# A two-layer decoder trunk on one core: the raw angle table moves from GpSimd to ScalarE, one projection block changes its PSUM bank, and the order of the recurrent heads is rewritten

## The reference, cut to what matters

```
h = rms_norm(x); proj = h @ w_in            # 1024 -> 512 (u) + 4 x 512 (q, f, i, g)
# mixer A: complex diagonal state space, 32 groups, a = exp(lambda * step)
bu = u @ bbar;  x_t = a * x_{t-1} + bu_t;  y = Re(C x) + d * u;  gelu(y) * sigmoid(gelu(y) @ w_glu)
# mixer B: 4 heads of gated linear recurrence, chunks of 32 tokens
f = lb + (1 - lb) * sigmoid(f);  k = 1 - f;  b = cumsum(log f) in the chunk
scores = (q exp(b - bref)) (k exp(bref - b))^T, causal;  u_chunk = (k exp(blast - b))^T v
state_c = exp(blast) state_{c-1} + u_chunk;  o = scores @ v + (q exp(b)) @ state_{c-1}
x = x + concat(A, rms_norm(o) * silu(g)) @ w_out
```

## Time and profile before

| | us |
|---|---|
| median of three executions | 835.0 (834.51 to 838.63) |
| the profiled execution, its own time | 837.01 |
| its span, first to last instruction | 835.3 |
| PE busy in the span | 773.3 |
| DVE / ACT / POOL busy | 608.6 / 499.8 / 166.1 |
| mean granted TensorE clock | 0.977 of full speed |

### The profile page before, as it was taken

The page is one execution under the profiler, slowest core; times in us unless marked ns, Lnnn a source line. Parts: engine busy times, 40 slices in busy tenths (PEclk is TensorE's granted clock), DMA queues, the critical chain, the costliest instruction groups (busy, mean ns, idle before and its releaser), DMA issues.

```text
span 835.3 us, 11410 instructions
## 1 busy us (share of the span) xinstructions
PE 773.3 (93%) x4356; PEld 579.2 (69%) x4356; DVE 608.6 (73%) x838; ACT 499.8 (60%) x664; POOL 166.1 (20%) x158
## 2 busy tenths in 40 slices
PE   6899999899999899988998999999999899999992
PEld 4587877454688778877876555556579778777771
DVE  5999785887553889887896466667635798787891
ACT  6458422923333488777885118677735488687881
POOL 5320010600001222322211001133101223222121
PEclk9899999999999999999999999999999899999998
DMA  9775554506452599989986300042063599999952
GB/s 368 175 170 128 107 155 85 114 2 252 201 213 116 181 420 362 320 316 327 319 301 217 132 0 1 25 177 101 1 277 151 202 408 352 313 322 329 311 195 39
DMA packets 35403, 170.91 MB, mean 205 GB/s; under 512 B 7841, under 2 KB 10017, under 8 KB 19728
## 3 DMA queue, kind: packets, MB, share of 16 engines
q1 hardware_dynamic: 18432, 130.03, 41.0%
q0 software_dynamic: 15184, 34.56, 17.2%
q10 hardware_dynamic: 1728, 5.52, 1.8%
HBM read 160.18 MB, written 24.12 MB: 221 GB/s over the span
## 4 chain that ended last, share of the span: by engine, by line
PE 42%; DMA 20%; DVE 19%; issue 7%; ACT 7%; POOL 2%; DVEq 1%; ACTq 0%; POOLq 0%
DMA ring<-stream 17%; DVE w_lo L1115 9%; PE PS L2184 8%; PE PS L2433 7%; PE PS L2314 4%; ACT w_hi L760 3%; PE PS L2339 3%; DMA ring_split<-stream 3%; PE PS L2468 2%; PE PS L2131 2%; PE PS L1972 2%; PE PS L1921 2%; DVE arena L1121 2%; PE PS L2214 1%; PE PS L2491 1%
## 5 line engine op out<-in xcount | busy, mean ns | idle before, releaser
L1115 DVE TENSOR_TENSOR w_lo<-ring,w_hi 128x2048 fp32r<-128x2048 f32 x92 | 210.0, 2288 | 41.8 <-ACT w_hi L760 38.0
L760 ACT ACTIVATE w_hi<-ring 128x2048 fp32r<-128x2048 f32 x86 | 164.5, 1916 | 45.1 <-DMA ring<-stream 40.9
L2314 PE MATMUL PS<-w_hi,left_hi 128*128 128x512 f32 x512 | 174.3, 402 | 7.5 <-DVE w_lo L1115 5.3
L2314 PEld LDWEIGHTS PS<-w_hi,left_hi 128*128 128x128 f32 x512 | 96.1, 188 | 30.5 <-DVE w_lo L1115 5.2
L2314 PE MATMUL PS<-w_lo,left_hi 128*128 128x512 f32 x256 | 100.1, 391 | 0.0
L2339 PE MATMUL PS<-w_hi,left_lo 128*128 128x512 f32 x256 | 86.6, 399 | 8.2 <-DVE left_lo L1115 7.0
L2433 PE MATMUL PS<-ring,hT 128*128 128x512 f32 (+1 forms) x192 | 74.7, 534 | 0.0
L608 POOL DMA_INDIRECT arena<-rows x32 | 41.0, 1281 | 125.5 <-PE PS L2291 112.1
L2339 PEld LDWEIGHTS PS<-w_hi,left_lo 128*128 128x128 f32 x256 | 48.8, 190 | 21.3 <-DVE left_lo L1115 9.6
L2433 PEld LDWEIGHTS PS<-ring,hT 128*128 128x128 f32 x192 | 35.2, 193 | 29.3 <-issue 27.6
L2314 PEld LDWEIGHTS PS<-w_lo,left_hi 128*128 128x128 f32 x256 | 48.3, 189 | 8.3
(11 more groups left out here) (301 smaller groups left out, 1479.2 us busy)
## 6 DMA issues: line engine op xcount, KB each, us to landing
ring<-stream SPq DMA_DIRECT2D x110, 1024.0 KB, 16.3
arena<-stream SPq DMA_DIRECT2D x6, 1024.0 KB, 8.2
ring_split<-stream POOLq DMA_DIRECT2D x11, 512.0 KB, 5.6
rows<-arena POOLq DMA_DIRECT2D x8, 512.0 KB, 3.0
x<-stream SPq DMA_DIRECT2D x4, 1024.0 KB, 6.4
x<-x_in SPq DMA_DIRECT2D x4, 512.0 KB, 5.2
ring_split<-stream POOLq DMA_DIRECT2D x2, 1024.0 KB, 8.9
left_lo<-hT_hi POOLq DMA_DIRECT2D x2, 1024.0 KB, 12.1
```

The lines of the kernel that those rows point to most:

```text
L760: act.activation(w_hi[pair], held_slot(layer, m), ACT.Copy).then_inc(w_hi_done, 1)
L1115: return V.tensor_tensor(out, a, b, op)
L2314: ins = mm(PS[:, gate_bank(e), :], a, b, start=k == 0 and t == 0, stop=k == KD - 1 and t == 2)
```

## The change

Four edits, all in layer 0's mixer.

1. The raw angle table is no longer one POOL product but 16 ACT copies of 128x128, each with a column of `turn_hi` as its scale. They stand behind `block_minus(4)` and in front of the evictions of u. DVE waits for `trig_done` instead of `turns_done`.
2. The fourth forget block (`split_proj(3)`) goes to PSUM bank 2 instead of 7 and waits for `u_done` 1 instead of `proj_done` 2. `inputs(0)`, which writes banks 0 to 3, now waits for `proj_done` 4. ACT evicts that block right behind the third, ahead of `block_hi(10)` and of the sine table.
3. PE's order in the second part: `make_taps` and `inputs(1)` one block sooner, `readout(1)` ahead of the last products of value blocks 8 and 9.
4. In the heads, PE runs `head_increments(h+1)` ahead of `head_out(h)`, ACT evicts the keys of head 0 ahead of the exponentials of head 3, and DVE keys head 2 ahead of `states(0)` and head 3 ahead of `states(1)`.

```diff
-            return 3 if i == 2 else 7 if i >= 14 else 6 + i % 2
+            return 5 - i if i in (2, 3) else 7 if i >= 14 else 6 + i % 2
...
-            nc.gpsimd.tensor_tensor(turn_lo, t3, turn_hi, ALU.subtract)
-            pool.drain()
+            nc.gpsimd.tensor_tensor(turn_lo, t3, turn_hi, ALU.subtract).then_inc(turns_done, 1)
             block_lo(1)
-            pool.wait_ge(const_rest, 48)
-            pool.wait_ge(turned_psum, 2 * TT)
...
-            nc.gpsimd.tensor_tensor(cosT.rearrange("p (i c) -> p i c", c=NSTEP), at_step,
-                                    turn_hi.unsqueeze(2).to_broadcast([P, PAIRS, NSTEP]), ALU.mult).then_inc(turns_done, 1)
...
+            act.wait_ge(turns_done, TURN_PARTS)
+            act.wait_ge(const_rest, 48)
+            act.wait_ge(turned_psum, 2 * TT)
+            for pair in range(PAIRS):
+                ins = act.activation(cosT[:, NSTEP * pair:NSTEP * (pair + 1)], con("time")[:, 0:NSTEP], ACT.Copy,
+                                     scale=turn_hi[:, pair:pair + 1])
+            ins.then_inc(trig_done, 1)
...
             projected(2)
+            projected(3)
             block_hi(10)
             block_minus(10)
...
             for h in range(HEADS):
                 exponentials(h)
-            keys_out(0)
+                if h == 2:
+                    keys_out(0)
...
-                if i >= 3:
+                if i >= 4:
                     pe.wait_ge(proj_done, i - 1)
-                if i == 2:
-                    pe.wait_ge(u_done, 2)
+                if i in (2, 3):
+                    pe.wait_ge(u_done, 4 - i)
...
-            pe.wait_ge(proj_done, 3)
+            pe.wait_ge(proj_done, 4)
             pe.wait_ge(bT_done, 2 * STEP)
             inputs(0)
             split_proj(4)
+            make_taps()
             split_proj(5)
-            make_taps()
+            inputs(1)
             split_proj(6)
-            inputs(1)
             split_proj(7)
...
             split_values(9, first)
+            readout(1)
             split_values(8, second)
             split_values(9, second)
-            readout(1)
```

More of the change, by code:

```diff
@@ L333, in trunk @@
                                                                sem("bT_psum"), sem("bT_done"))
-        TURN, RAW = 1, 2
-        TRIG, LB, TABLE = 1, 2, 3
+        TURN, TURN_PARTS = 1, 2
+        TRIG, LB, RAW, TABLE = 1, 2, 3, 4
         BOUNDS, HT_HI, HT_LO, IN_COEF, PHASE, READ_COEF = 1, 2, 3, 5, 6, 7
@@ L555, in _ @@
             pool.drain()
-            nc.gpsimd.tensor_tensor(turn_lo, t3, turn_hi, ALU.subtract)
-            pool.drain()
+            nc.gpsimd.tensor_tensor(turn_lo, t3, turn_hi, ALU.subtract).then_inc(turns_done, 1)
             block_lo(1)
-            pool.wait_ge(const_rest, 48)
-            pool.wait_ge(turned_psum, 2 * TT)
-            at_step = con("time")[:, 0:NSTEP].unsqueeze(1).to_broadcast([P, PAIRS, NSTEP])
-            nc.gpsimd.tensor_tensor(cosT.rearrange("p (i c) -> p i c", c=NSTEP), at_step,
-                                    turn_hi.unsqueeze(2).to_broadcast([P, PAIRS, NSTEP]), ALU.mult).then_inc(turns_done, 1)
             for j in range(2, 12):
@@ L886, in values_hi @@
                 act.activation(v_lo(half), v_hi(half), ACT.Copy, scale=-1.0).then_inc(in_split, 1)
-            for i in range(3, 12):
+            block_hi(11)
+            block_minus(11)
+            for i in range(4, 12):
                 projected(i)
-                if i == 3:
-                    block_hi(11)
-                    block_minus(11)
                 if i in (5, 7):
@@ L1278, in _ @@
             grown(in_b, in_re, in_im, in_tmp, STEP - 1, ALU.subtract, ALU.add).then_inc(coefs_done, 1)
-            dve.wait_ge(turns_done, RAW)
+            dve.wait_ge(trig_done, RAW)
             at_step = con("time")[:, 0:NSTEP].unsqueeze(1).to_broadcast([P, PAIRS, NSTEP])
@@ L1449, in _ @@
             causal(0)
+            keyed(2)
+            decayed(2)
             for h in range(HEADS):
@@ L1453, in _ @@
                     causal(h + 1)
-                if h + 2 < HEADS:
-                    keyed(h + 2)
-                    decayed(h + 2)
+                if h == 0:
+                    keyed(3)
+                    decayed(3)
                 if h:
@@ L2142, in _ @@
             proj(14, low)
+            head_increments(1)
             head_out(0)
-            head_increments(1)
             head_scores(2)
             proj(14, high)
+            head_increments(2)
             head_out(1)
-            head_increments(2)
             head_scores(3)
             proj(15, low)
+            head_increments(3)
             head_out(2)
-            head_increments(3)
             proj(15, high)
```

## The result

The changed kernel takes **826.6 us** (median of four runs, 826.5 to 826.8) against 836.8 us for the kernel before, timed beside it on the same chip (median of four, 834.5 to 838.6): a ratio of 0.988, 95% interval 0.985 to 0.991. The profiled executions say the same: a span of 824.9 us in place of 835.3, an own time of 826.6 in place of 837.0. The forecast was 824.0 with a range of 820 to 830.5.

The account below looks back on a forecast made before the run. PE, busy 93% of the span, was the bound, so gains come from its waits and low clock: 3.3 + 2.9 + 1.2 + 0.95 + 3.0 = 11.4 us off, forecast 824.0 us, range 820 to 830.5.

Parts of the forecast that it names:

- Edit 1: u blocks: without POOL's product `left_lo` comes earlier, 3.3 us, and the clock stays full, 2.9 us; together 6.2 us.
- the point of 33.38 us: u blocks: the moment `left_lo`'s second half arrived in the earlier trace; PE was to pass it at 30.1, 3.3 us sooner.
- Edit 2: Fourth forget block: the 2.04 us wait at `split_proj(3)` goes, `inputs(0)` waits instead; 1.2 us won, bounds nothing and 2.0.
- The late sine table: Ahead of `inputs(1)`: table 4.1 us later, PE still not waiting, by 0.9 us; rival, PE waits, 1 to 3 us, chance 0.06.
- Edit 3: Value blocks 8 and 9: `readout(1)` covers the 1.0 us wait for their low part; 0.95 us won.
- Edit 4: Heads: PE begins `glu` at 198.4 instead of 201.38; 3.0 us won, bounds nothing and 4.5.
- the second way: Heads: waits of 6.7 us become about 5 and 1.7 us of low clock goes; 3.4 us won.
- The clock rivals: u blocks or heads: waits still bring half clock, 827 to 829, chance 0.16; heads staying slow, about 850, chance 0.04.
- All of it reaches the end: Behind the mixer: PE's progress starts the expert weight transfers, so every microsecond won by 218 us reaches the end.
- The sum of 11.4 us: Whole kernel: 3.3 + 2.9 + 1.2 + 0.95 + 3.0 us won, all in layer 0's mixer.
- all 31.9 us of the heads' work at half speed: Heads: the slower case's extreme, clock falling and not rising before `glu`; about 850 us, chance 0.04.
- the good bounds of edits 2 and 4: Fourth forget block and heads: at best 2.0 and 4.5 us won, given as 820.5 us.

Follow-up runs that it names:

- e1_table_only: The kernel before with edit 1 alone (angle table by ACT copies): 830.9 us, ratio 0.991 to 0.997.
- e5_pe_filler: The kernel before plus 22 transposes on PE during its wait for `left_lo`, POOL's table product kept: ratio 0.997 (0.995 to 1.000).
- e12_no_new_order: The changed kernel with edit 3 undone: 824.7 us, ratio 0.982 to 0.993.
- e7: The changed kernel with DVE's old order in the heads: 823.2 us, ratio 0.979 to 0.984.
- e6_pe_heads_old: The changed kernel with PE's old order in the heads (`head_out` ahead of the next increments): 829.0 us, ratio 0.987 to 0.992.
- e9: The kernel before with edit 1 and 16 extra transposes filling PE's wait ahead of `split_proj(3)`: 829.0 us, ratio 0.991 to 0.998.
- e11: The kernel before with edits 1 and 2 only: 829.5 us, ratio 0.988 to 0.995.
- e8: The changed kernel with ACT's old order in the heads (keys of head 0 behind all exponentials): 823.3 us, ratio 0.980 to 0.992.
- e4: The changed kernel with the angle table back on POOL as one product, placed behind `left_lo`: 825.9 us, ratio 0.985 (0.982 to 0.987).
- e10: The changed kernel with DVE's old order in the heads and ACT's gate evictions ahead of head 3's exponentials: 823.8 us, ratio 0.979 to 0.985.
- e3_heads_only: The kernel before with edit 4 alone (order in the heads): 833.6 us, ratio 0.994 to 1.000.

## Why the prediction was right, step by step

**Edit 1: 3.3 us of stall and 2.9 of clock, 6.2; measured 5.6.** Mechanism and place were right: the four products take 0.43 us at 23.92 in place of 3.86, `left_lo` starts at 25.20 (forecast 25.6), and the clock is 1.00 behind the wait. Counted from the first u product, the point of 33.38 us comes 8.10 us behind it in place of 11.01, 2.9 us sooner; and the stage's rest is 2.7 us shorter, the clock. The 0.4 us missing of the stall is a wait of 1.01 us where 0.7 was foreseen: PE began 0.7 us sooner in this execution, DVE only 0.2. The copies took 4.78 us for the 4.8 of the forecast, and PE waited for none of the evictions behind them.

What the prediction did not see is that edit 1 alone can give back 1.6 us at `split_proj(3)`, as it did in the execution of `e1_table_only` (and the filler in `e5_pe_filler`). It took the 1.00 at the 2.0 us wait as a property of that wait. That the sum came out all the same is luck in this point: edit 2 takes the wait away, and with edit 1 alone the same reasoning was wrong by 1.6 us.

**Edit 2: 1.2 us; measured 1.5.** `inputs(0)` waits 0.73 us, the forecast was 0.75. The wait removed was worth 2.29 us from `turn_inputs` to `split_proj(3)` (5.70 to 3.41), not 2.04: PE's start behind a wait costs some tenths too. The late sine table behaved as computed: DVE issued the last of `products_in(1)` by 79.25 + 2.48 = 81.73 us, 15.7 us behind `inputs(0)` (forecast 15.85), and `inputs(1)` came at 83.06, with 1.3 us to spare. That rival did not come about.

**Edit 3: 0.95 us; measured 1.2, and 1.8 by taking it back.** The low part's DMA would have been waited for by 1.6 us in the changed kernel (`e12_no_new_order`), longer than the 1.0 of the earlier trace rows.

**Edit 4: 3.0 us (3.4 by the second way); measured 3.4.** The four waits were foreseen as 0.9, 0.5, 1.75 and 1.6 and are 0.77, 0.62, 1.71 and 1.56. `states(0)` to `states(3)` start 0.5, 1.7, 4.7 and 6.3 us sooner relative to projection 12, for 0.4, 1.3, 4.2 and 5.5. That `states(0)` gains almost nothing was right as well; the prediction stated it as a fact of the change and did not ask what the keying in front costs, and `e7` shows it is 1.5 us.

**The clock rivals.** Neither the 1.0 us wait nor the four of the heads brought the clock down: 1.00 from 150 to 189 us, where the earlier trace rows had 0.59 in one stretch. The Trainium skill, "TensorE: Matmul & The Clock Gate", section "A second HAM failure mode: psum-queue depth-cycling", describes a clock that swings between its two levels when PE is idle for short times between groups of products, often enough; it gives no length for them. In the changed kernel the clock did not swing. In `e6_pe_heads_old`, behind waits of 1.71 us at 157.87 and 1.55 at 163.09, it was 0.83 for 10 us. Waits of the same length stand in the same place in the changed kernel, so the rule does not tell the two apart here.

**All of it reaches the end: not quite.** This is the step that was wrong, by 2.1 us. At the output products PE was 12.5 us ahead, in the end 10.4. The first 1.3 us are lost in the router stage, where PE never waits for long. PE's timeline of the last group of router products and the transposes behind it, before:

```profile
271.70 4.07 PE L2214 MATMUL PS<-param,arena 128*128 128x20 f32 x32
...
278.29 1.29 PE L2247 MATMUL PS<-const 128*128 128x128 f32 x10
```

and in the changed kernel:

```profile
259.17 5.29 PE L2218 MATMUL PS<-param,arena 128*128 128x20 f32 x32
...
267.09 1.58 PE L2251 MATMUL PS<-const 128*128 128x128 f32 x10
```

The work is the same, and the clock was 0.52 for 6 us of it. In the kernel before it was low there too, but less so:

```profile
268.00:276.00 8.00, 8.00 (x68) 7.91 (x67) 6.06 (x12) 4.52 (x7) 1.45 (x3) 0.92 0.60 235
276.00:282.00 6.00, 4.79 (x46) 4.17 (x44) 5.06 (x22) 3.00 (x2) 1.06 (x2) 0.82 0.53 211
```

Length times missing clock gives 1.7 us there and 3.4 in the changed kernel, enough for the 1.3. In the other kernels this stage takes between 68.9 and 70.4 us, and what lies behind it between 543.9 and 549.2 (543.9, 544.0 and 545.5 in `e9`, `e1` and `e11`, 547.0 or more in all others), with no order that the edits explain: `e12`, whose router stage took 69.3 us, and `e8`, 68.9, differ from the changed kernel only in what happens some 60 us earlier and more. I can't say what sets it, and behind the router stage it is not the clock alone: what a low clock costs there, summed over stretches of 10 us, is 8.6 us in the kernel before, 8.5 in the changed one, 8.0 in `e1` (which is 4 to 5 us shorter there) and 6.9 in `e4` (which is as long as the changed one). The spread is as large as an edit of this change, which is the likely reason why the heads' orders and edit 3, which stand clear of each other in their stages, hardly do in the medians.

The sum of 11.4 us was thus met by 11.8 us won in the mixer (without the earlier start), and 2.1 lost behind it.

Two figures of the prediction do not follow from its own terms; neither bears on the sum. With all 31.9 us of the heads' work at half speed the time would be 823.9 + 31.9, some 856 us, unless the slower work filled waits, and not 850. And the good bounds of edits 2 and 4, 0.8 and 1.5 us beyond the sum, lead to 821.6, not to 820.5.

## What to carry to other kernels

Before an edit is priced at what its wait costs, look for what the same idle time costs in clock behind it, and price edits that touch neighbouring waits together: here one was worth 1.5 us alone and 3.1 behind another, in the executions profiled. When an order is changed on several engines at once, take each engine's part back by itself; in this change PE's part was worth 4.5 us, DVE's cost 1.5 and ACT's was worth 0.2. And judge edits of 1 to 2 us by the stage in which they act, because the length of the later stages varies by more than that from kernel to kernel (543.9 to 549.2 us behind the router) for reasons that the edits don't explain.

The fastest by its median is `e7_dve_heads_old`, the changed kernel without DVE's new order: 823.2 us, 0.981 of the time before (0.979 to 0.984). `e8`, `e10` and `e12` lie within 1.5 us of it, so that the order among them is not shown.

## What the runs showed of the hardware that was not expected

- The same wait of 2.04 us, behind the same 32 transposes, left TensorE's clock at 1.00 in the kernel before (and the stage at its full speed in `e3_heads_only`, 11.40 us), and brought it to 0.77 over the 7.3 us behind it in `e1_table_only` (and 0.77 in `e5_pe_filler`, 1.6 us in both). In the first two the clock had been low 30 us earlier, in the last two it had not. Four kernels show this, one execution each; nothing that was tried explains it, and chance is not ruled out.
- Four waits of 0.77, 0.62, 1.71 and 1.56 us within 11 us left the clock at 1.00 (changed kernel); one wait of 3.70 us at the same place brought 0.69 and 0.88 over the 8.6 us behind it (`e8_keys_late`), as the 3.7 us of the earlier trace rows were followed by 0.59. How low it is differs behind the same wait: the 30 increments behind it took 1.47 to 2.09 us in the six kernels with the old orders in the heads.
- The clock also fell where PE was busy without a gap: 0.52 over 262 to 268 us of the changed kernel, with 6.00 us busy of 6, among products of 20 columns and transposes. It had been 0.89 over the 5 us ahead, with 5.00 us busy of 5.
